# Attention of the second stack: the order of VectorE's steps within a unit

## The chip, the cores and the metric

The kernel runs on one core of one Trainium2 chip. The metric is the device time of one execution in microseconds (us); lower is better.

## What is computed

A two-layer network (the first stack) is followed by a second two-layer stack with latent attention (MLA). Everything is float32; D_MODEL is 1024, there are 256 tokens of the stream and 256 of a context. The part around the change is the attention of the second stack, eight heads, with 64 plain and 32 rotated features in queries and keys and 64 value features:

```python
def attend(q_nope, q_rope, k_nope, k_rope, v):
    s = (jnp.einsum("bqhd,bkhd->bhqk", q_nope, k_nope)
         + jnp.einsum("bqhr,bkr->bhqk", q_rope, k_rope)).astype(jnp.float32) * ATTN_SCALE
    p = jax.nn.softmax(s, axis=-1).astype(v.dtype)
    return jnp.einsum("bhqk,bkhd->bqhd", p, v)
```

In both layers the 256 stream queries attend to stream and context keys together (512 keys). In layer 0 the 256 context queries also attend to the 256 context keys. The result, with a Fourier part and a convolution part, is multiplied by w_out.

## The kernel before

Every engine has its own hand-written, in-order program, and the programs meet through semaphores (`event(...)` and a few others), on whose counts the waits stand. The network is a list of stages. A `Linear` stage streams weight tiles from HBM through a ring of four buffers; ScalarE makes the upper half of a weight (`w_hi`, line 2132), VectorE the rest (`w_lo`, line 2343), and TensorE (PE in the profile) adds three products (line 1896). VectorE makes `w_lo` of the tile that is AHEAD = 3 places ahead (`split`).

The stage `("mla", layer)` computes attention in **units**. A unit is one head with all 256 queries (two tiles of 128) against 512 keys (a long unit) or 256 keys (a short unit). `mla_units` (line 1572) gives layer 0 eight long units and then eight short ones, and layer 1 eight long ones. Layer 0's stage lies at about 1324 to 1378 us of the trace and layer 1's at about 2231 to 2266 us. For unit i the steps are these:

- scores: `mla_scores`, TensorE, line 1633, into two of the four PSUM banks of the weight ring. It waits until the exponents of unit i - 2, which used the same banks, are done.
- maxima: `mla_maxima`, VectorE, lines 1730 and 1732: two row maxima from PSUM, then a small multiplication that makes the bias of the exponents.
- exponents: `exps`, ScalarE, line 1703: two activations that also sum the rows. Each is an ACTIVATE and an ACTIVATION_READ_ACCUMULATOR. They wait for the maxima of unit i.
- scalings: `probabilities`, VectorE, lines 1742 and 1745: the reciprocals of the sums, and two multiplications in place.
- turning: `middle`, TensorE, line 1661: transposes of the weights into PSUM banks 4 and 5, which are single: it waits for the scalings of unit i and for both copies of unit i - 1.
- copies: half of the turned weights by ScalarE (line 1722), half by VectorE (line 1758), both after the turning.
- values: `pair_values`, TensorE, line 1674, once per pair of units, after both copies of the second. Then ScalarE takes the upper half (line 1718) and VectorE the rest (line 1763, the low halves).

TensorE's queue is, for i from 1 on: scores of unit i + 1, for odd i >= 3 the values of pair (i - 3) / 2, turning of unit i - 1. With the last units come four parts of the output product (`mixed_part`, line 1896 again): part 0 before the turning of the last unit but one, part 1 before the turning of the last unit, then part 2, the last values, and part 3. ScalarE's queue (`mla_scalar`, from line 1695) is: exponents of unit i, upper half of a pair, copy of unit i - 1. VectorE's queue is written out in `mla_vector` (line 1734): scalings of unit i - 1, maxima of unit i + 1, copy of unit i - 1, low half of a pair. The scores and maxima of unit 0 are made in the stage before.

Of the kernel before, what the change touches and what calls it, by code (L numbers as in the profile page):

```python
# [360 lines left out]
def build(nc, dram, out, stages):  # L361
# [4 lines left out]
    with ExitStack() as stack:  # L366
# [163 lines left out]
        def event(name):  # L530

            if name not in done:
                done[name] = sem(name)
            return done[name]
# [5 lines left out]
        def cols(c):  # L540
            return slice(c * T, (c + 1) * T)
# [3 lines left out]
        def link(eng, ins, who):  # L545

            steps[who][1] += 1
            ins.then_inc(steps[who][0], 1)
            eng.wait_ge(*steps[who])
# [810 lines left out]
        def mixed_rows(st):  # L1360

            return h_one[0] if st[1] else (h_hi, h_lo)
# [209 lines left out]
        def mla_units(st):  # L1572

            units = [(h, 0, 0, 2 * T) for h in range(HEADS)]
            return units + ([(h, T, T, T) for h in range(HEADS)] if st[1] == 0 else [])

        def mla_base(st):
            return 0 if st[1] == 0 else 16
# [38 lines left out]
        def score_bank(st, i, t):  # L1617

            return (tiles_before(st) + 2 * (i % 2) + t) % RING
# [104 lines left out]
        def mla_maxima(dve, st, i):  # L1724

            V = nc.vector
            nk = mla_units(st)[i][3]
            dve.wait_ge(event("mla_scores"), mla_base(st) + i + 1)
            for t in range(NT):
                last = V.tensor_reduce(stat2[:, i, t:t + 1], ps[:, score_bank(st, i, t), 0:nk], AX_X, ALU.max)  # L1730
            link(dve, last, "dve")
            V.tensor_scalar(stat2[:, i, 2:4], stat2[:, i, 0:2], -MLA_SCALE, None, ALU.mult).then_inc(event("mla_max"), 1)

        def mla_vector(dve, st, split):
            V = nc.vector
            units, b0 = mla_units(st), mla_base(st)
            n = len(units)

            def probabilities(i):
                _, _, _, nk = units[i]  # L1740
                dve.wait_ge(event("mla_exps"), b0 + i + 1)
                link(dve, V.reciprocal(stat2[:, i, 6:8], stat2[:, i, 4:6]), "dve")
                for t in range(NT):
                    p = p2[:, i % 2, t, 0:nk]
                    last = V.tensor_scalar(p, p, stat2[:, i, 6 + t:7 + t], None, ALU.mult)
                last.then_inc(event("mla_probs"), 1)

            for i in range(n + 2):
                if 1 <= i < n + 1:
                    probabilities(i - 1)  # L1750
                if i + 1 < n:
                    mla_maxima(dve, st, i + 1)
                if i == n - 1:
                    split(stages[stages.index(st) + 1], AHEAD)
                if 1 <= i < n + 1:
                    nk = units[i - 1][3]
                    dve.wait_ge(event("mla_turned"), b0 + i)
                    V.tensor_copy(pt2[:, (i - 1) % 3, 0:nk // P, P:T], ps[:, 5, 0:nk].rearrange("p (k n) -> p k n", n=P)).then_inc(event("mla_copied_dve"), 1)
                if i >= 3 and i % 2:
                    b = (i - 3) // 2  # L1760
                    dve.wait_ge(event("mla_hi"), b0 // 2 + b + 1)
                    d = (slice(None), 4 + b % 4, cols(b // 4))
                    V.tensor_tensor(mixed_rows(st)[1][d], ps[:, 6 + b % 2, 0:T], mixed_rows(st)[0][d].bitcast(F32), ALU.subtract).then_inc(s_h, 1)
# [572 lines left out]
        def _(dve):  # L2336
# [274 lines left out]
            for st in stages:  # L2611
# [127 lines left out]
                elif st[0] == "attention":  # L2739
                    attention_vector(dve, st)  # L2740
                elif st[0] == "delta":
                    delta_vector(dve, st, split)
                elif st[0] == "mixer":
                    mixer_vector(dve, st)
                elif st[0] == "mla":
                    mla_vector(dve, st, split)
# [43 lines left out]
```

## Time and profile before

| | us |
|---|---|
| median of 3 runs | 2485.19 |
| lowest and highest | 2482.44 and 2488.31 |
| the profiled execution: its own time | 2484.83 |
| the profiled execution: its span | 2483.0 |
| mean granted TensorE clock in it | 0.996 |

The span is the time from the first to the last instruction that the profile shows; 1.83 us of the execution's time lie around it. In rows of the timeline the first number is the start in us from the span's start, the second the duration in us, then follow engine, line, operation, output and inputs, and in brackets the engine's idle time before it with what ended it.

### The profile page before, as it was taken

How to read it: one execution, taken by the hardware profiler on the slowest of the kernel's cores; microseconds unless marked ns; L12 is line 12 of the kernel's file. 1: busy time of each engine (PE TensorE's matmuls, PEld its weight loads, DVE VectorE, ACT ScalarE, POOL GpSimd, SP SyncE). 2: the span in 40 equal slices, each digit the busy share in tenths (PEclk: the TensorE clock that was granted, in tenths of full speed). 3: DMA queues.
4: the chain of work that ended last, by engine and by line, in shares of the span. 5: the costliest groups of instructions: out<-in, count | busy, mean ns of one | idle time of the engine just before them, and what ended most of it. 6: DMA issues, size and time to landing. Idle time of an engine off the chain costs nothing.

```text
span 2483.0 us, 37020 instructions
## 1 busy us (share of the span) xinstructions
PE 2416.5 (97%) x14770; PEld 2095.3 (84%) x14770; DVE 1761.1 (71%) x3048; ACT 1058.0 (43%) x1684; POOL 59.8 (2%) x56
## 2 busy tenths in 40 slices
PE   6999999999999999999999999999999999999998
PEld 4869999977999988888886888888888888877998
DVE  3668889965778777677768676666866565877666
ACT  4556447742644522222536442222532222555444
POOL 0110001022000000000000000000000000000000
PEclk9999999999999999999999999999999999999999
DMA  8567885533666445554311244444354444432553
GB/s 306 211 249 247 288 273 177 179 136 136 215 210 205 159 163 186 175 181 153 105 36 64 77 153 163 159 166 155 104 180 151 152 144 129 126 102 94 186 184 125
DMA packets 113675, 409.93 MB, mean 165 GB/s; under 512 B 12640, under 2 KB 20064, under 8 KB 108896
## 3 DMA queue, kind: packets, MB, share of 16 engines
q1 hardware_dynamic: 113504, 407.56, 48.6%
q8 instruction: 118, 1.93, 0.3%
q14 instruction: 53, 0.43, 0.0%
HBM read 406.46 MB, written 1.05 MB: 164 GB/s over the span
## 4 chain that ended last, share of the span: by engine, by line
PE 90%; DVE 5%; ACT 2%; DMA 2%; issue 1%; SPq 0%; POOL 0%; DVEq 0%; ACTq 0%
PE ps L1896 77%; PE ps L1918 2%; DVE w_lo L2343 1%; PE ps L605 1%; PE ps L911 1%; DMA first_high<-in_first_rows 1%; PE ps L1674 1%; PE ps L921 1%; PE ps L1661 1%; PE ps L1633 1%; PE ps L1936 1%; ACT w_hi L2132 0%; DVE ssq L2498 0%; DMA raw<-in_tiles 0%; DVE x L2475 0%
## 5 line engine op out<-in xcount | busy, mean ns | idle before, releaser
L2132 ACT CAST w_hi<-raw 128x1024 fp32r<-128x1024 f32 (+3 forms) x557 | 555.1, 997 | 1126.1 <-PE ps L1896 1105.3
L1896 PE MATMUL ps<-h_hi,w_hi 128*128 128x258 f32 (+2 forms) x2928 | 962.5, 329 | 13.4 <-DVE h_lo L2568 4.3
L1896 PE MATMUL ps<-h_lo,w_hi 128*128 128x258 f32 (+2 forms) x2928 | 951.5, 325 | 0.0
L1896 PE MATMUL ps<-h_hi,w_lo 128*128 128x258 f32 (+2 forms) x2928 | 950.4, 325 | 0.0
L2343 DVE TENSOR_TENSOR w_lo<-raw,w_hi 128x1024 fp32r<-128x1024 f32 (+3 forms) x557 | 645.9, 1160 | 273.3 <-ACT w_hi L2132 269.5
L1896 PEld LDWEIGHTS ps<-h_hi,w_hi 128*128 128x128 f32 x2928 | 553.8, 189 | 67.2 <-issue 11.1
L1896 PEld LDWEIGHTS ps<-h_hi,w_lo 128*128 128x128 f32 x2928 | 553.5, 189 | 49.1 <-issue 3.6
L1896 PEld LDWEIGHTS ps<-h_lo,w_hi 128*128 128x128 f32 x2928 | 553.1, 189 | 45.3
L1896 PE MATMUL ps<-a_hi,w_hi 128*128 128x256 f32 (+1 forms) x1056 | 353.5, 335 | 0.5 <-DVE a_lo L2388 0.5
L1896 PE MATMUL ps<-a_hi,w_lo 128*128 128x256 f32 (+1 forms) x1056 | 353.1, 334 | 0.0
L1896 PE MATMUL ps<-a_lo,w_hi 128*128 128x256 f32 (+1 forms) x1056 | 353.1, 334 | 0.0
L1896 PEld LDWEIGHTS ps<-a_lo,w_hi 128*128 128x128 f32 x1056 | 199.9, 189 | 20.5
L1896 PEld LDWEIGHTS ps<-a_hi,w_hi 128*128 128x128 f32 x1056 | 198.2, 188 | 21.7 <-DVE a_lo L2388 1.1
L1896 PEld LDWEIGHTS ps<-a_hi,w_lo 128*128 128x128 f32 x1056 | 198.2, 188 | 20.7
L2360 DVE SCALAR_TENSOR_TENSOR ada_raw<-ada_raw,cond_rows 128x1024 f32<-128x1024 f32 x160 | 195.1, 1219 | 0.0
L2475 DVE SCALAR_TENSOR_TENSOR x<-ps,coef,x 128x256 f32<-128x256 f32 x256 | 116.0, 479 | 96.3 <-PE ps L1896 96.3
L2360 DVE SCALAR_TENSOR_TENSOR ada_acc<-ada_raw,cond_rows 128x1024 f32<-128x1024 f32 x128 | 155.8, 1217 | 0.0
L2463 DVE TENSOR_TENSOR a_f<-silu_g,ps 128x512 f32<-128x512 f32 x64 | 44.0, 687 | 98.0 <-PE ps L1896 61.0
L2439 DVE TENSOR_TENSOR normed<-ps,rstd 128x258 f32<-128x258 f32 x165 | 69.8, 423 | 40.6 <-PE ps L1896 36.2
L2388 DVE TENSOR_TENSOR a_lo<-a_f,a_hi 128x256 fp32r<-128x256 f32 (+1 forms) x132 | 72.9, 552 | 12.0 <-ACT a_hi L2165 12.0
L2165 ACT CAST a_hi<-a_f 128x256 fp32r<-128x256 f32 (+1 forms) x132 | 67.1, 509 | 12.6 <-DVE a_f L2443 12.0
L2191 ACT ACTIVATE h_hi<-x,coef 128x256 fp32r<-128x256 f32 x72 | 34.9, 506 | 28.0 <-DVE x L2475 27.8
(369 smaller groups left out, 2135.7 us busy)
## 6 DMA issues: line engine op xcount, KB each, us to landing
raw<-in_tiles SPq DMA_DIRECT2D x477, 512.0 KB, 3.8
ada_raw<-in_w_mod_by_feature SPq DMA_DIRECT2D x128, 512.0 KB, 3.6
wide_rows<-in_wide_rows SPq DMA_DIRECT2D x32, 1024.0 KB, 4.9
raw<-in_tiles SPq DMA_DIRECT2D x48, 384.0 KB, 3.1
ada_raw<-in_ada_w_by_feature SPq DMA_DIRECT2D x32, 512.0 KB, 4.4
first_low<-in_first_rows SPq DMA_DIRECT2D x2, 2048.0 KB, 13.3
first_high<-in_first_rows SPq DMA_DIRECT2D x2, 2048.0 KB, 21.9
raw<-in_tiles SPq DMA_DIRECT2D x16, 192.0 KB, 2.3
```

The lines of the kernel that those rows point to most:

```text
L605: last = nc.tensor.matmul(ps[32 * j:32 * j + 32, bank, :], cond_wide[:, k, :], wide_one[i % 2][:, HALF * j:HALF * (j + 1)], start=(k == 0) ...
L1896: last = mm(ps[0:m, slot, 0:n], w[:, slot, k * P:k * P + m], v[:, s0 + k, c0:c0 + n], start=(k == 0 and w is w_hi and v is hi), stop=(k == ...
L1918: last = mm(to, w[:, slot, k * P:(k + 1) * P], v[:, k, c * W:(c + 1) * W], start=(k == 0 and w is w_hi and v is hi), stop=(k == KD - 1 and ...
L2132: nc.scalar.copy(w_hi[:, slot, 0:n], raw[:, slot, 0:n]).then_inc(s_hi, 1)
L2165: nc.scalar.copy(a_hi[:, j // 2, a0:a0 + n], a_f[:, (j // 2) % 2, 0:n]).then_inc(s_ahi, 1)
L2191: A(hi[:, j, 0:T], x[:, j, cols(c)], ACT.Identity, scale=coef[:, c, 0, j:j + 1]).then_inc(event("scaled_hi"), 1)
L2343: V.tensor_tensor(w_lo[:, slot, 0:n], raw[:, slot, 0:n], w_hi[:, slot, 0:n].bitcast(F32), ALU.subtract).then_inc(s_lo, 1)
L2360: last = V.scalar_tensor_tensor(out=junk if unit >= SECOND and c == 0 else rows, in0=rows, scalar=1.0, in1=cond_rows[:, c], op0=ALU.mult, ...
L2388: V.tensor_tensor(a_lo[:, pair, a0:a0 + n], a_f[:, pair % 2, 0:n], a_hi[:, pair, a0:a0 + n].bitcast(F32), ALU.subtract).then_inc(s_alo, 1)
L2439: V.tensor_tensor(z, ps[:, slot, 0:W], rstd_2[:, 0], ALU.mult).then_inc(s_evac, 1)
L2463: V.tensor_tensor(a_f[:, pair % 2, 0:n], silu_g[:, pair % 2, 0:n], bank, ALU.mult).then_inc(s_evac, 1 if lin.more["early"] and pair == 1 e ...
L2475: last = V.scalar_tensor_tensor(out=x[:, j, cols(c)], in0=ps[:, slot, cols(c)], scalar=coef[:, c, 2, j:j + 1], in1=x[:, j, cols(c)], op0=A ...
```

## The change

Only the order of VectorE's queue within the attention stage changes. The maxima of unit 1 stay first. Then, in step i, the scalings of unit i (before: of unit i - 1) stand ahead of the maxima of unit i + 1, and the copy of unit i - 1 and the low half come behind them as they did. The scalings of the last unit so come ahead of the `split` of the weight tile instead of behind it.

```diff
+            mla_maxima(dve, st, 1)
             for i in range(n + 2):
-                if 1 <= i < n + 1:
-                    probabilities(i - 1)
-                if i + 1 < n:
+                if i < n:
+                    probabilities(i)
+                if i and i + 1 < n:
                     mla_maxima(dve, st, i + 1)
                 if i == n - 1:
                     split(stages[stages.index(st) + 1], AHEAD)
```

No instruction is added or removed and no transfer is changed. The queues of TensorE, ScalarE and SyncE are untouched.

## Rows read from the trace of the kernel before

**Rows 1.** The page, busy time of each engine.
```profile
PE 2416.5 (97%) x14770; PEld 2095.3 (84%) x14770; DVE 1761.1 (71%) x3048; ACT 1058.0 (43%) x1684; POOL 59.8 (2%) x56
```

**Rows 2.** Waits, 1324 to 1372 us: total, times, longest.
```profile
PE ps L1661 <- DVE p L1745: 4.1, 6, 1.2
```

**Rows 3.** Waits, 2231 to 2263 us, the same columns.
```profile
PE ps L1661 <- DVE p L1745: 1.5, 3, 0.7
```

**Rows 4.** Timeline, long units, PE, ACT and DVE, 1335 to 1344 us.
```profile
1335.33 1.09 PE L1661 MATMUL ps<-consts,p 128*128 128x128 f32 x8
...
1336.94 0.69 ACT L1703 ACTIVATE p<-ps,rstd 128x512 f32<-128x512 f32 x1
...
1337.40 0.15 DVE L1742 RECIPROCAL rstd<-rstd 128x2 f32<-128x2 f32 x1
...
1337.59 0.88 DVE L1745 TENSOR_SCALAR p<-p,rstd 128x512 f32<-128x512 f32 x2
...
1338.18 0.21 ACT L1703 ACTIVATION_READ_ACCUMULATOR p<-ps,rstd 128x1 f32 x1
1338.39 1.28 DVE L1730 TENSOR_REDUCE rstd<-ps 128x1 f32<-128x512 f32 x2
...
1338.53 1.09 PE L1661 MATMUL ps<-consts,p 128*128 128x128 f32 x8 [0.39 <-DVE p L1745]
...
1339.70 0.17 DVE L1732 TENSOR_SCALAR rstd<-rstd 128x2 f32<-128x2 f32 x1
...
1343.15 1.09 PE L1661 MATMUL ps<-consts,p 128*128 128x128 f32 x8
```

**Rows 5.** Timeline, short units, PE, ACT and DVE, 1361 to 1367 us.
```profile
1361.95 0.66 PE L1661 MATMUL ps<-consts,p 128*128 128x128 f32 x4
...
1362.92 0.48 ACT L1703 ACTIVATE p<-ps,rstd 128x256 f32<-128x256 f32 x1
...
1363.73 0.21 ACT L1703 ACTIVATION_READ_ACCUMULATOR p<-ps,rstd 128x1 f32 x1
...
1364.18 0.66 PE L1661 MATMUL ps<-consts,p 128*128 128x128 f32 x4 [0.70 <-DVE p L1745]
...
1365.23 0.16 DVE L1742 RECIPROCAL rstd<-rstd 128x2 f32<-128x2 f32 x1
...
1365.95 0.75 DVE L1730 TENSOR_REDUCE rstd<-ps 128x1 f32<-128x256 f32 x2
...
1366.65 0.66 PE L1661 MATMUL ps<-consts,p 128*128 128x128 f32 x4
1366.74 0.17 DVE L1732 TENSOR_SCALAR rstd<-rstd 128x2 f32<-128x2 f32 x1
```

**Rows 6.** Timeline of ScalarE: exponents of units 1 and 15, then layer 1's 1 and 7.
```profile
1327.44 0.69 ACT L1703 ACTIVATE p<-ps,rstd 128x512 f32<-128x512 f32 x1
...
1369.84 0.48 ACT L1703 ACTIVATE p<-ps,rstd 128x256 f32<-128x256 f32 x1
...
2234.01 0.69 ACT L1703 ACTIVATE p<-ps,rstd 128x512 f32<-128x512 f32 x1
...
2254.52 0.69 ACT L1703 ACTIVATE p<-ps,rstd 128x512 f32<-128x512 f32 x1
```

**Rows 7.** Timeline of TensorE at the end of layer 1's stage.
```profile
2254.95 1.95 PE L1674 MATMUL ps<-pt,v_tok 128*64 128x256 f32 x16 [0.95 <-ACT pt L1722]
...
2261.48 1.09 PE L1661 MATMUL ps<-consts,p 128*128 128x128 f32 x8 [0.68 <-DVE p L1745]
```

**Rows 8.** Timeline of TensorE, two of its longer waits elsewhere.
```profile
390.79 0.39 PE L1896 MATMUL ps<-h_hi,w_hi 128*128 128x258 f32 x1 [1.77 <-DVE h_lo L2568]
...
621.98 0.36 PE L1896 MATMUL ps<-h_hi,w_hi 128*128 128x256 f32 x1 [2.22 <-DVE h_lo L1302]
```

**Rows 9.** Busy time by engine in a stretch; the number after POOL's is the granted clock.
```profile
390.00:395.00 5.00, 3.98 (x16) 3.60 (x17) 3.48 (x8) 3.52 (x6) 0.00 (x0) 0.66 0.61 180
620.00:625.00 5.00, 3.02 (x25) 3.04 (x26) 3.97 (x13) 2.31 (x4) 0.00 (x0) 1.00 0.00 0
```

## The prediction

> **What bounds the kernel now.** I read the page first. TensorE is busy for 97% of the span [rows 1], so outside a few places everything else hides behind it, and a change that touches only VectorE's queue can act only where TensorE waits. The waits of the two attention stages come next. What ends TensorE's idle time there is mostly the scaling of the exponents, for which the turning waits: 4.1 us in layer 0 [rows 2] and 1.5 us in layer 1 [rows 3]. Those 5.6 us are what an earlier scaling could give back at most. The timeline shows how they come about. Between two turnings behind values, that is one pair of long units, lie 1343.15 - 1335.33 = 7.82 us, of which TensorE waits 0.39 [rows 4]; a pair of short units takes 1366.65 - 1361.95 = 4.70 us with a wait of 0.70 [rows 5]. So the period is 3.91 us per long unit and 2.35 us per short one, set by TensorE's own work and a short detour: turning, copy, scaling, turning. The maxima are not on that path, since they stand one unit ahead of the scalings in VectorE's queue.
>
> **What the order changes.** Instructions and durations stay. What matters is a dependence that the new order closes. The exponents of unit i + 1 need its maxima; the maxima of unit i + 1 now stand on VectorE behind the scalings of unit i; and these need the exponents of unit i. Every unit thus runs through exponents, scalings, maxima, exponents, with ScalarE and VectorE by turns and neither ahead of the other. Before, the maxima of unit i + 1 stood behind the scalings of unit i - 1 only, one unit of slack.
>
> **The length of this loop, long unit** [rows 4]. Exponents: from 1336.94 to the end of the second sum, 1338.18 + 0.21 = 1338.39, so 1.45 us. Reciprocal and scalings: from 1337.40 to the start of the next instruction, 1338.39, so 0.99. Maxima: from 1338.39 to 1339.70 + 0.17, so 1.48. Two handoffs between engines; the nearest price is scaling to turning, from 1337.59 + 0.88 = 1338.47 to 1338.53, 0.06 each, and I take 0.05. Sum 1.45 + 0.99 + 1.48 + 0.10 = 4.02 us, against 3.91 now: 0.11 more per unit.
>
> **Short unit** [rows 5]. Exponents 1363.73 + 0.21 - 1362.92 = 1.02; scalings 1365.95 - 1365.23 = 0.72; maxima 1366.74 + 0.17 - 1365.95 = 0.96; handoffs 0.10. Sum 2.80 us, against 2.35: 0.45 more per unit.
>
> **Layer 0.** The loop starts at the exponents of unit 1, at 1327.44, which nothing in the change moves: maxima 1 and scalings 0 keep their order, and the exponents wait for ScalarE's own queue. Those of unit 15 start at 1369.84 now, 42.40 us later [rows 6]. The new way has seven steps out of a long unit and seven out of a short one: 7 x 4.02 + 7 x 2.80 = 47.74 us, 5.34 more. Carrying the three queues forward unit by unit gives two additions. For units 4, 6 and 8 ScalarE is still at its copy when the maxima are ready (about 0.06 each, 0.2 in all). At unit 10, just after the change to short units, the long values of pair 3 come late, ScalarE stands behind them with the upper half and a copy, and the loop is held once for about 0.7 us. So unit 15 starts at about +6.2. The output product's first part begins behind the values of pair 6, which wait for VectorE's copy of unit 13; that copy now stands behind the maxima of unit 15, so it comes as late as they do and hands the +6.2 on. From there TensorE runs back to back as before.
>
> **Layer 1.** Unit 1 starts at 2234.01 and unit 7 at 2254.52, 20.51 us later [rows 6]. Now 6 x 4.02 plus 0.12 for units 4 and 6 = 24.24, 3.7 more. The values of pair 2, which wait 0.95 us for a copy now [rows 7], wait for VectorE's copy of unit 5, behind the maxima of unit 7, and carry the delay on, about +3.8. Then comes a gain: the last turning waits 0.68 us for scalings [rows 7], which now stand ahead of the split and the copy and are long done. Net about +3.1.
>
> **What costs nothing.** The maxima of unit 1 were first in the queue already. The split of the weight tile now stands behind the last scalings; its tile is first read by part 3 of the output product, three parts and two turnings later, and that slack covers a delay of about 1 us. If it did not, each microsecond of it would be one on TensorE. The weight load that waits for this split moves with it; no queue of transfers is otherwise passed. Late next are VectorE's copies: the one of unit i - 1 comes behind the maxima of unit i + 1, so it starts no sooner than 0.05 + 0.99 + 1.48 = 2.5 us after the exponents of unit i end, and TensorE's turning or values wait for it. In this loop TensorE has 7.82 - 0.39 = 7.43 us of work in 8.04, so it has room.
>
> **The clock.** The new gaps of TensorE are longer: carried forward, about 2.3 us ahead of the values of pair 6 in layer 0, about 2.6 ahead of those of pair 2 in layer 1, others 1.6 or less. Elsewhere in this trace a wait of 1.77 us is followed by a stretch at 0.66 granted clock, hence partly at the 1.2 GHz level, and a wait of 2.22 us by none [rows 8, 9]. In the first case 5 us at 0.66 are 5 x 0.34 = 1.7 us of lost full speed. Both long gaps lie just ahead of product parts, where TensorE is the bound, so a fall would be paid. I put one such fall, 1.7 us, into the forecast; none and two are its bounds. The Trainium skill (TensorE: Matmul & The Clock Gate, What's actually happening) says that the throttled state is the default and activity releases it; the first of the two rows agrees, the second does not show it.
>
> **Sum.** 6.2 + 3.1 + 1.7 = 11.0 us. Against the profiled execution's own time this gives 2484.83 + 11.0 = 2495.8; the median of the runs shown is 0.36 higher, within their spread, so I say 2496.
>
> **The rivals.**
> *TensorE stays the bound and the change pays* (faster). Its 7.43 us of work per long pair are near the loop's 8.04, and if the maxima did not hold the exponents, the 5.6 us of waits for scalings would go: 2484.83 - 5.6 = 2479.2. It decides if the loop is shorter than TensorE's work alone, 3.72 us long and (4.70 - 0.70) / 2 = 2.00 us short. The rows give 4.02 and 2.80, so what speaks for it is only that I could have misread a dependence. The Trainium skill (Perfetto Trace Analysis, Optimization Strategy) advises to find the gaps of the contended engine and make what it waits for start sooner, which is what the change does for the scalings; the trace shows such gaps, and the rule says nothing of what is then late.
> *Only the short units lose* (no change). If the long units' loop were covered, by handoffs near nothing, long units would stay at 3.91 and only 7 x 0.45 = 3.2 remain; less the 0.7 at the end of layer 1, 2487.3.
> *TensorE's clock falls often.* With gaps of over 1 us in nearly every pair the lower level might come back again and again. Six falls at 1.7 us instead of one add 8.5: 2504. Against it: the gaps of some 1 us [rows 7] are there now, with a mean granted clock of 0.996 over the whole execution, and part of such a loss would hide behind the loop.
> *The change does not do what it says.* The queues are in order and the loop is written out, so I give this 1 in 100: 2485.
>
> **How the numbers follow.** Forecast 0.85, faster 0.03, only the short units 0.06, many falls 0.05, no effect 0.01. The forecast's own bounds: no fall of the clock (-1.7), two (+1.7), handoffs of 0.03 to 0.08 in 20 steps with two each (-0.8, +1.2), the additions of the carried-forward queues absent or doubled (-0.9, +0.9), and 2 us of scatter of a median either way. I take 2490 to 2502. A measurement of this kernel tells about 0.2%, 5.0 us, from no change; above it lie all but the low end of the forecast and the falls of the clock: slower 0.88. Within it lie the short-units case, the low end and no effect: 0.09. Faster 0.03.
>
> **What the new profile would show.** In steady long units the exponents start every 4.0 to 4.1 us and in short ones every 2.8; each starts within 0.1 us of the end of its maxima, and each reciprocal within 0.1 us of the end of the exponents. VectorE waits for ScalarE's exponents in every unit. TensorE's wait for scalings is gone and replaced by one for VectorE's copy (line 1758). The turning that waited 0.68 us at the end of layer 1 waits no longer. The stretch from the exponents of unit 1 to the output product is 6 us longer in layer 0 and nearly 4 in layer 1; the rest of the trace only moves. Wrong would be: a period of 3.9 us or less in long units, exponents that start long after their maxima, or a time that differs outside the two stages.

## The result, and the profile of the changed kernel

| | before | changed |
|---|---|---|
| median, us | 2485.17 (6 runs, 2482.44 to 2488.31) | 2497.63 (6 runs, 2494.84 to 2499.27) |
| the profiled execution's own time | 2484.83 | 2498.75 |
| span | 2483.0 | 2497.0 |
| mean granted clock | 0.996 | 0.994 |

The changed kernel takes 1.0045 times as long, with a 95% interval of 1.0036 to 1.0055. By the medians that is 12.5 us more. The page shows the same work as [rows 1]; only the span has grown:

```profile
PE 2420.0 (97%) x14770; PEld 2098.7 (84%) x14770; DVE 1764.1 (71%) x3048; ACT 1059.5 (42%) x1684; POOL 60.3 (2%) x56
```

Line numbers behind line 1747 are up by one; the copy of VectorE is now line 1759 and the product line 1897. The waits from 1324 to 1385 us show what the two engines do now (engine and line, then who is waited for, total, times, longest):

```profile
ACT p L1703 <- DVE rstd L1732: 11.6, 10, 2.1
DVE rstd L1742 <- ACT p L1703: 11.6, 15, 1.6
...
PE ps L1674 <- issue: 6.9, 5, 2.1
...
PE ps L1674 <- DVE pt L1759: 2.1, 2, 1.2
PE ps L1661 <- DVE pt L1759: 1.8, 3, 1.2
```

ScalarE waits for the maxima and VectorE for the exponents, each 11.6 us in all, and neither wait stood in the list of before. TensorE no longer waits for the scalings as in [rows 2]. Its waits now stand mostly ahead of values, 9.0 us in all. For 2.1 us of them the profile names VectorE's copy; for the other 6.9 it names nothing (`issue`), and there the timeline has to tell what ended them (below). The timeline of one long unit in steady state answers to [rows 4]:

```profile
1342.20 0.69 ACT L1703 ACTIVATE p<-ps,rstd 128x512 f32<-128x512 f32 x1
...
1343.45 0.21 ACT L1703 ACTIVATION_READ_ACCUMULATOR p<-ps,rstd 128x1 f32 x1
1343.69 0.17 DVE L1742 RECIPROCAL rstd<-rstd 128x2 f32<-128x2 f32 x1 [0.79 <-ACT p L1703]
...
1344.69 1.28 DVE L1730 TENSOR_REDUCE rstd<-ps 128x1 f32<-128x512 f32 x2
1346.01 0.17 DVE L1732 TENSOR_SCALAR rstd<-rstd 128x2 f32<-128x2 f32 x1
...
1346.21 0.69 ACT L1703 ACTIVATE p<-ps,rstd 128x512 f32<-128x512 f32 x1 [1.30 <-DVE rstd L1732]
```

The sums of the exponents end at 1343.66 and the reciprocal starts at 1343.69. The bias of the next exponents ends at 1346.18 and those exponents start at 1346.21. From unit 4 to unit 5 it is one chain without slack, 1346.21 - 1342.20 = 4.01 us from one unit's exponents to the next's. In front of units 4, 6 and 8 there is a little more: ScalarE is still at its copy when the bias is ready, and the step is 4.15 to 4.19 us. A pair of long units so takes 8.20 us, against 7.82 before. Two short units answer to [rows 5]:

```profile
1370.39 0.47 ACT L1703 ACTIVATE p<-ps,rstd 128x256 f32<-128x256 f32 x1 [0.30 <-DVE rstd L1732]
...
1371.44 0.17 DVE L1742 RECIPROCAL rstd<-rstd 128x2 f32<-128x2 f32 x1 [0.43 <-ACT p L1703]
...
1373.16 0.47 ACT L1703 ACTIVATE p<-ps,rstd 128x256 f32<-128x256 f32 x1 [1.30 <-DVE rstd L1732]
```

The step is 2.77 us, but for one of 3.50 into unit 10. The exponents of unit 1 and unit 15 in layer 0 and of units 1 and 7 in layer 1 answer to [rows 6]:

```profile
1330.02 0.69 ACT L1703 ACTIVATE p<-ps,rstd 128x512 f32<-128x512 f32 x1
...
1378.70 0.47 ACT L1703 ACTIVATE p<-ps,rstd 128x256 f32<-128x256 f32 x1 [1.30 <-DVE rstd L1732]
...
2243.03 0.69 ACT L1703 ACTIVATE p<-ps,rstd 128x512 f32<-128x512 f32 x1
...
2267.42 0.69 ACT L1703 ACTIVATE p<-ps,rstd 128x512 f32<-128x512 f32 x1 [1.31 <-DVE rstd L1732]
```

I call the two distances the **stretches**: 48.68 us in layer 0 and 24.39 in layer 1, against 42.40 and 20.51 before. They are taken inside one execution, so what scatters elsewhere does not touch them.

The loop costs most where it starts. In the kernel before, the exponents of units 2 and 3 followed fast, 5.05 us for both in either layer, since the maxima of a unit did not have to wait for the exponents of the one ahead of it. Here are those of layer 1's unit 3, before and changed, 5.05 and 7.99 us behind unit 1:

```profile
2239.06 0.69 ACT L1703 ACTIVATE p<-ps,rstd 128x512 f32<-128x512 f32 x1
```

```profile
2251.02 0.69 ACT L1703 ACTIVATE p<-ps,rstd 128x512 f32<-128x512 f32 x1 [1.60 <-DVE rstd L1732]
```

The stretch is 3.88 us longer in layer 1 and 6.28 in layer 0, and 2.94 us of either are the loss of this head start. The longer steps of the later units give the rest.

Last, TensorE at the end of layer 1's stage, which answers to [rows 7], and the granted clock there:

```profile
2267.29 0.69 DVE L1759 COPY pt<-ps 128x512 f32<-128x512 f32 x1
...
2268.08 3.63 PE L1674 MATMUL ps<-pt,v_tok 128*64 128x256 f32 x16 [2.59 <-issue]
...
2275.46 1.03 PE L1661 MATMUL ps<-consts,p 128*128 128x128 f32 x8
```

```profile
2265.00:2270.00 5.00, 2.41 (x15) 1.68 (x15) 3.97 (x11) 2.03 (x5) 0.00 (x0) 0.82 0.01 3
2270.00:2275.00 5.00, 5.00 (x38) 3.98 (x35) 1.89 (x3) 0.96 (x2) 0.00 (x0) 0.84 0.29 105
```

The wait ahead of the values of pair 2 is 2.59 us. It ends 0.10 us behind VectorE's copy of unit 5 (2267.29 + 0.69 = 2267.98), which stands behind the maxima of unit 7. Behind this wait the clock falls: the values take 3.63 us instead of 1.95, and 5 x (0.18 + 0.16) = 1.7 us of full speed are lost. The last turning waits no longer.

**Where the 13.9 us between the two profiled executions lie.** Up to the exponents of unit 1 in layer 0 the changed kernel is 2.58 us later (1330.02 against 1327.44), before any changed instruction. In layer 0, from there to the last turning, it takes 6.40 us more (56.13 against 49.73). Between the stages 0.04. In layer 1, from the exponents of unit 1 to the last values, 4.89 more (34.83 against 29.94). The rest, 0.1, lies behind. So the change costs 11.3 us here, and 2.6 are scatter of an earlier part.

### The profile page after: what moved, and what is told of

Its sections match the earlier page's. It is cut to its first block, busy times and chain, and to the rows that moved or that the text cites. A ratio compares the mean times of both kernels' runs of the same rounds, so it can differ in the third digit from the quotient of the medians.

```text
span 2497.0 us, 37020 instructions
## 1 busy us (share of the span) xinstructions
PE 2420.0 (97%) x14770; PEld 2098.7 (84%) x14770; DVE 1764.1 (71%) x3048; ACT 1059.5 (42%) x1684; POOL 60.3 (2%) x56
## 3 DMA queue, kind: packets, MB, share of 16 engines
q8 instruction: 118, 1.93, 0.3%
## 4 chain that ended last, share of the span: by engine, by line
PE 89%; DVE 5%; ACT 2%; DMA 2%; issue 1%; SPq 0%; POOL 0%; DVEq 0%; ACTq 0%
PE ps L1897 77%; PE ps L1919 2%; DVE w_lo L2344 1%; PE ps L605 1%; DMA first_high<-in_first_rows 1%; PE ps L911 1%; PE ps L1674 1%; PE ps L921 1%; PE ps L1937 1%; ACT p L1703 1%; PE ps L1661 0%; ACT w_hi L2133 0%; DMA raw<-in_tiles 0%; DVE rstd L1730 0%; DVE ssq L2499 0%
```

## Experiments

The rivals to the loop theory were these: TensorE's work or the clock sets the stages; the late copies of VectorE are the cause; scaling a unit early costs in whatever order. In each profile I read the two stretches; times are medians, and the kernel before ran on the same chips: 2486.61 us beside the first four kernels and 2486.55 beside the second four.

**One: maxima ahead of scalings.**

```diff
             mla_maxima(dve, st, 1)
             for i in range(n + 2):
-                if i < n:
-                    probabilities(i)
                 if i and i + 1 < n:
                     mla_maxima(dve, st, i + 1)
+                if i < n:
+                    probabilities(i)
```

> From the changed kernel, only the maxima of unit i + 1 and the scalings of unit i change places: the maxima no longer stand behind scalings that wait for the exponents of unit i; VectorE's copy stays behind both. Loop theory (exponents, scalings, maxima, exponents by turns): the loop is open, so the stretch from the exponents of unit 1 to those of unit 15 in layer 0 falls from 48.7 us to about 42.2 (42.4 in the kernel before), that from unit 1 to unit 7 in layer 1 from 24.4 to about 20.7, and the time is about 1 us above the kernel before, 2486. Rival, late copies (it is VectorE's copy behind maxima and scalings that holds TensorE): the copy is as late as in the changed kernel, so the stretches stay near 48 and 24 us and the time near 2495 to 2498.

Measured: 2489.09 us, 1.0009 of the kernel before (1.0000 to 1.0019). Its exponents of units 1 and 15 in layer 0:

```profile
1327.16 0.69 ACT L1703 ACTIVATE p<-ps,rstd 128x512 f32<-128x512 f32 x1
...
1369.86 0.47 ACT L1703 ACTIVATE p<-ps,rstd 128x256 f32<-128x256 f32 x1 [0.18 <-DVE rstd L1732]
```

The stretches are 42.70 and 20.95 us (2234.90 to 2255.85 in layer 1). Two steps changed places, and 6.0 of the 6.3 us of layer 0's stretch came back, although the copy still stands behind both. The late copies are not what makes the stretch long. They do make gaps at its end: in layer 1 the values of pair 2 waited 2.34 us, and the clock fell behind that wait as well (0.88 and 0.78 in the two 5 us from 2255, 1.7 us of full speed). With the 0.7 us of the stretches that would account for the 2.5 us by which this kernel's median is above the kernel before; about 1 had been expected.

**Two: copy ahead of maxima.**

```diff
                 if i < n:
                     probabilities(i)
-                if i and i + 1 < n:
-                    mla_maxima(dve, st, i + 1)
-                if i == n - 1:
-                    split(stages[stages.index(st) + 1], AHEAD)
                 if 1 <= i < n + 1:
                     nk = units[i - 1][3]
...
+                if i and i + 1 < n:
+                    mla_maxima(dve, st, i + 1)
+                if i == n - 1:
+                    split(stages[stages.index(st) + 1], AHEAD)
```

> From the changed kernel, VectorE's copy of unit i - 1 moves ahead of the maxima of unit i + 1, behind the scalings of unit i. Loop theory: the copy (0.61 us long, 0.34 short) and its wait for the turning come into the loop, so it gets longer: unit 1 to 15 in layer 0 from 48.7 to about 54 us, unit 1 to 7 in layer 1 from 24.4 to about 27.8, time about 15 us over the kernel before, plus what the clock takes: 2500 to 2503. Late copies: the copy comes 1.4 us earlier in every unit and TensorE's waits for it go, so most of the loss comes back: 2486 to 2490.

Measured: 2505.04 us, 1.0076 (1.0060 to 1.0092). Exponents of units 1 and 15 in layer 0:

```profile
1329.03 0.69 ACT L1703 ACTIVATE p<-ps,rstd 128x512 f32<-128x512 f32 x1
...
1383.67 0.47 ACT L1703 ACTIVATE p<-ps,rstd 128x256 f32<-128x256 f32 x1 [1.82 <-DVE rstd L1732]
```

Stretches of 54.64 and 27.59 us. The copy comes earlier than in the changed kernel and the kernel is slower still, since the copy and its wait for the turning now lie in the loop. The theory of the late copies is out. The time lies 2 us above the expected range although the stretches are as expected; the clock fell behind waits of TensorE at the end of both stages here too (2.43 us in layer 0, 3.48 in layer 1).

**Three and four: a third row maximum, in the changed kernel and in the kernel before.** Both add one line in `mla_maxima`; its result is overwritten by the reciprocal later.

```diff
+            V.tensor_reduce(stat2[:, i, 6:7], ps[:, score_bank(st, i, 0), 0:nk], AX_X, ALU.max)
             for t in range(NT):
                 last = V.tensor_reduce(stat2[:, i, t:t + 1], ps[:, score_bank(st, i, t), 0:nk], AX_X, ALU.max)
```

> The changed kernel with one more row maximum per unit (of tile 0, into a column that the reciprocal overwrites later), about 0.64 us in a long unit and 0.37 in a short one. Loop theory: every microsecond of it lies in the loop: unit 1 to 15 in layer 0 from 48.7 to about 54.5 us, unit 1 to 7 in layer 1 from 24.4 to about 28.0, time about 9.7 us over the changed kernel, 2507. Theory that TensorE's work or its clock sets the stages: the addition is largely hidden, under 3 us.

> The kernel before with the same additional maximum. Loop theory: here the maxima stand a unit ahead and only part of the addition comes through, where VectorE is late with the scalings: unit 1 to 15 in layer 0 from 42.4 to about 44.7 us, unit 1 to 7 in layer 1 from 20.5 to about 22.0, time about 4 us over the kernel before, 2489. If VectorE's work as such bounded both kernels, the addition would cost as much as in the changed kernel, some 10 us.

Measured: 2510.50 us with it in the changed kernel, 12.9 over that kernel's median, and 2489.95 in the kernel before, 3.3 over its own (1.0013, 1.0003 to 1.0022). The exponents of units 1 and 7 in layer 1, first in the changed kernel with the addition, then in the kernel before with it:

```profile
2252.54 0.69 ACT L1703 ACTIVATE p<-ps,rstd 128x512 f32<-128x512 f32 x1
...
2280.12 0.69 ACT L1703 ACTIVATE p<-ps,rstd 128x512 f32<-128x512 f32 x1 [2.21 <-DVE rstd L1733]
```

```profile
2236.86 0.69 ACT L1703 ACTIVATE p<-ps,rstd 128x512 f32<-128x512 f32 x1
...
2258.61 0.69 ACT L1703 ACTIVATE p<-ps,rstd 128x512 f32<-128x512 f32 x1 [0.26 <-DVE rstd L1733]
```

In layer 1 the stretch grew by 27.58 - 24.39 = 3.19 us in the changed kernel and by 21.75 - 20.51 = 1.24 in the kernel before. In layer 0 it grew by 8.65 (57.33) and 1.93 (44.33). So the same addition to VectorE's work costs the stretch 2.6 times as much under the new order in layer 1. Layer 0's ratio of 4.5 holds more than the loop: its 57.33 is 2.8 over what I expected. There TensorE's waits ahead of values had grown to 1.81 and 2.32 us, and the granted clock was lower over twenty microseconds:

```profile
1350.00:1360.00 10.00, 7.68 (x40) 5.05 (x38) 7.22 (x17) 4.34 (x11) 0.00 (x0) 0.84 0.00 0
1360.00:1370.00 10.00, 8.51 (x54) 6.00 (x51) 7.28 (x23) 3.76 (x12) 0.00 (x0) 0.86 0.00 0
```

A slower TensorE makes the copies late enough to hold ScalarE. That this is the whole 2.8 us was not tested.

**Five and six: a product part in the gap, in the changed kernel and in the kernel before.** On TensorE the first part of the output product moves ahead of the values of the last pair but one.

```diff
+                if i == n - 1:
+                    mixed_part(0)
                 if i >= 3 and i % 2:
                     pair_values((i - 3) // 2)
-                if n - 1 <= i < n + 1:
-                    mixed_part(i - n + 1)
+                if i == n:
+                    mixed_part(1)
```

> The changed kernel, with the first part of the output product moved on TensorE ahead of the values of the last pair but one, so that it fills the gap in which TensorE waits for VectorE's copy. Clock theory: in layer 1 that gap falls from 2.6 us to about 1.1, the granted clock stays at full through the end of the stage (0.86 in the changed kernel), and the values of that pair take 1.95 us instead of 3.63; with 3.5 us of filled gaps in both layers the time is about 5 us under the changed kernel, 2492 to 2493. Loop theory beside it: the stretches of the exponents stay at 48.7 and 24.4 us. Rival: the clock falls here for another reason; then the clock stays at about 0.86 and only 3.5 us or less are won, 2494 or more.

> The same move in the kernel before, where the gap is 0.95 us in layer 1 and some 0.6 in layer 0 and the clock stays up: about 1.8 us under the kernel before, 2484 to 2485, with unchanged stretches of 42.4 and 20.5 us. If the move helped by itself and not by filling the gap, it would win as much as in the changed kernel, some 5 us.

Measured: in the changed kernel 2491.30 us, 6.3 under its median (1.0025 of the kernel before, 1.0013 to 1.0036; by the two ratios the move wins 0.0020, or 5.0 us); in the kernel before 2483.99 us, 2.6 under it (0.9991, 0.9982 to 1.0000, so at the edge of what can be told from no change). The values of pair 2 in layer 1 and the clock behind them, in the changed kernel with the move:

```profile
2265.21 1.95 PE L1674 MATMUL ps<-pt,v_tok 128*64 128x256 f32 x16 [1.16 <-issue]
```

```profile
2265.00:2270.00 5.00, 4.79 (x42) 4.18 (x43) 3.29 (x7) 1.96 (x6) 0.00 (x0) 1.00 0.17 36
```

The wait is 1.16 us instead of 2.59, the clock stays full and the values take 1.95 us instead of 3.63. The stretches are unchanged in both kernels: 48.67 and 24.38, and 42.40 and 20.52. So the loop and the clock are two separate costs: the loop is as it was, and the fall of the clock went with the long wait. The trace is of one execution, but the medians agree with it: had the clock fallen all the same, 3.5 us or less were to be won. From unit 1 to the last values layer 1 takes 31.65 us instead of 34.83, and layer 0's way to the last turning 54.20 instead of 56.13, 5.1 less in all, as expected.

**Seven: maxima, copy, scalings, low half**, on top of the move of experiment six. The diff is against the changed kernel. Written out as one row, the queue of the kernel before is maxima of unit i + 1, copy of unit i - 1, in every second step a low half, scalings of unit i. The change puts these scalings ahead of all three, experiment one ahead of copy and low half, this one ahead of the low half alone. So they do not come as early as in the change, though the expectation says so. At the end of the stage copy and scalings also pass the split.

```diff
             mla_maxima(dve, st, 1)
             for i in range(n + 2):
-                if i < n:
-                    probabilities(i)
                 if i and i + 1 < n:
                     mla_maxima(dve, st, i + 1)
-                if i == n - 1:
-                    split(stages[stages.index(st) + 1], AHEAD)
                 if 1 <= i < n + 1:
                     nk = units[i - 1][3]
...
+                if i < n:
+                    probabilities(i)
+                if i == n - 1:
+                    split(stages[stages.index(st) + 1], AHEAD)
```

> From the kernel of the part in the gap, VectorE's order within a step is maxima of unit i + 1, copy of unit i - 1, scalings of unit i, low half: scalings a unit early as in the change, but behind the maxima, so that the loop is open, and behind the copy, for which TensorE waits. Loop theory with the queues carried forward: unit 1 to 15 in layer 0 41.1 us (42.4 before), unit 1 to 7 in layer 1 20.1 (20.5), and with the filled gaps about 4.3 us under the kernel before, 2482; TensorE then waits next to nowhere for scalings or copies in long units. Rival: early scalings are what costs, in whatever order; then the stretches are above 44 and 22 us and the time is above the kernel before.

Measured: 2481.98 us, 0.9983 of the kernel before (0.9974 to 0.9992), the fastest of all and 2.0 us under experiment six. Exponents of units 1 and 15 in layer 0 (two lines further down in this kernel):

```profile
1329.22 0.69 ACT L1705 ACTIVATE p<-ps,rstd 128x512 f32<-128x512 f32 x1
...
1370.41 0.48 ACT L1705 ACTIVATE p<-ps,rstd 128x256 f32<-128x256 f32 x1
```

Stretches of 41.19 and 19.95 us, both shorter than before. TensorE's waits for scalings from 1324 to 1372 us are 2.0 us, half of [rows 2]:

```profile
PE ps L1661 <- DVE p L1747: 2.0, 4, 0.9
```

Scaling earlier is thus no cost in itself; what counts is what the scalings pass. Both stretches together, against the kernel before: past the low half 1.8 us are won, past the copy too (experiment one) 0.7 are lost, past the maxima too (the change) 10.2.

**Eight: the changed order in layer 1 only.**

```diff
-            mla_maxima(dve, st, 1)
+            if st[1] == 1:
+                mla_maxima(dve, st, 1)
             for i in range(n + 2):
-                if i < n:
-                    probabilities(i)
-                if i and i + 1 < n:
+                u = i if st[1] == 1 else i - 1
+                if 0 <= u < n:
+                    probabilities(u)
+                if (i or st[1] == 0) and i + 1 < n:
                     mla_maxima(dve, st, i + 1)
```

> The changed order in layer 1's attention stage alone, the order before in layer 0's. Loop theory: unit 1 to 15 in layer 0 42.4 us as before, unit 1 to 7 in layer 1 24.4 as changed, time about 3.1 us over the kernel before, and 1.7 more where the clock falls there: 2490. A theory that the two stages do not add up (that layer 0's delay causes the one of layer 1, or the clock's fall) expects 20.5 in layer 1 and no fall of the clock, 2486.

Measured: 2491.75 us, 1.0022 (1.0012 to 1.0031), 5.2 us over the kernel before; expected were 4.8. The stretches are 42.40 in layer 0, to the hundredth that of before, and 24.39 in layer 1, to the hundredth that of the changed kernel. The clock falls there again:

```profile
2263.26 3.32 PE L1674 MATMUL ps<-pt,v_tok 128*64 128x256 f32 x16 [2.59 <-issue]
```

Layer 1's cost needs no delay in layer 0, and the two add up.

## Why the prediction was right

**The loop.** It said that exponents, scalings, maxima and the next exponents become one chain: shown by the timeline and by experiments one, two, three and four. Every unit was to start within 0.1 us of the end of its maxima; units 4, 6 and 8 start some 0.2 us behind it. Its terms were 4.02 us per long unit, measured 4.01, and 2.80 per short one, measured 2.77. The handoffs between ScalarE and VectorE, taken as 0.05 us each, measure 0.03 in the long unit shown.

**The two stages.** Layer 0 was to take 6.2 us more and took 6.40. The stretch is 6.28 us longer, and two of the terms in it were off in opposite ways. The steps alone give 7 x 4.01 + 7 x 2.77 = 47.46, 5.06 over 42.40, where 5.34 had been put in; ScalarE at its copy adds 0.5 where 0.2 had been; the hold at unit 10, put at 0.7, is 3.50 - 2.77 = 0.73. So the sum is nearer than its terms, by luck. Another point is easily misread. The prediction gives 0.11 us more per long unit and 0.45 per short one, which would be 3.9 us in layer 0 and 0.7 in layer 1. It is right all the same, since it took its additions from the whole stretches, and these hold the head start of units 2 and 3, which it never names. Layer 1 was to take 3.1 us more without the clock and took 4.89 with it; less the 1.7 us of the clock that is 3.2.

**The clock.** One fall, 1.7 us, had been put in. It came in layer 1, behind a wait of 2.59 us (forecast 2.6), and not in layer 0, whose longest wait in the stage was 2.10 (forecast 2.3). That it would be one, and not none or two, was a choice between bounds and no forecast from a mechanism. Experiment five ties the fall to the wait. The Trainium skill (TensorE: Matmul & The Clock Gate, What's actually happening) says that the throttled state is the default and activity releases it; the trace agrees, with 1.00 behind the wait of 1.16 us and 0.82 and 0.84 from the one of 2.59 us on.

**What was covered.** The split behind the last scalings cost nothing, as said. Part 3 of the product, which reads its tile, starts 4.32 us behind the last turning in layer 0 in both kernels (1390.47 - 1386.15 and 1381.49 - 1377.17), and in layer 1 1.88 us behind the last values against 1.87. From the exponents of unit 15 to the last turning layer 0 takes 7.45 us against 7.33.

**The sum.** 11.0 us was forecast and the profiled executions give 11.3 in the two stages; the medians differ by 12.5, and the interval, 1.0036 to 1.0055 or 8.9 to 13.7 us, holds both. What the prediction had only in its bounds, as 2 us either way, is the scatter that lies ahead of the stages, 2.58 us in the profiled execution.

**The rivals.** TensorE stays the bound: out, for the stretches follow VectorE's queue (experiment three) and not TensorE's. Only the short units lose: out, since layer 1 has long units alone and lost 3.2 us beside the clock. The clock falls often: it did so only in kernels whose loop is longer still. The change does not do what it says: out by the timeline. The hope behind the faster case was real, though. Experiment seven, which holds the move of experiment six, wins 4.6 us by the medians; 42.40 - 41.19 + 20.51 - 19.95 = 1.8 us of that lie in the stretches, which experiment six left as they were. They come from the scalings as well, moved past the low half and not past the maxima.

## What to carry to other kernels

When an instruction that waits for an engine stands in the queue ahead of one that this same engine waits for, the two form a circle. What counts is over how many units it closes. In the kernel before, the maxima of unit i + 1 stood behind the scalings of unit i - 1, and so the same durations, 4.02 us by the prediction's sum, closed only every second unit: about 2.0 us per unit (an estimate, 4.02 / 2), well under TensorE's 3.91. In the changed kernel they close in every unit, the engines run by turns however much slack each has by itself, and 4.01 to 4.19 us replace the 3.91. Any head start that one engine had built up is lost besides, here 2.94 us in each layer. Before moving a step earlier in an in-order queue, write down for every step behind it who waits for it, add up the circle and divide by its units. Where two steps may both come early, put first the one whose input is ready without the other engine.

## What the runs showed of the hardware

The same wait at the same place can bring a fall of the granted clock in one execution and none in another. Behind a wait of 2.22 us at 621.98 the kernel before kept 1.00 [rows 8, 9]; the changed kernel, with the same instructions there and a wait of 2.23 us, had less:

```profile
622.74 0.37 PE L1897 MATMUL ps<-h_hi,w_hi 128*128 128x256 f32 x1 [2.23 <-DVE h_lo L1302]
```

```profile
620.00:625.00 5.00, 2.77 (x16) 2.60 (x15) 4.14 (x12) 1.24 (x2) 0.00 (x0) 0.79 0.00 0
625.00:630.00 5.00, 5.00 (x39) 5.00 (x38) 3.83 (x6) 4.34 (x7) 0.00 (x0) 0.86 0.20 60
```

The two executions were 0.76 us apart at that wait and 2.58 us apart at the first attention stage. This one fall, 5 x (0.21 + 0.14) = 1.75 us, is nearly all of what came on between.

The traces of all ten kernels hold the instructions of this early part, unchanged. In the 10 us from 2 us before the instruction at which the wait ends:

| wait of TensorE, us | near | fell to 0.83 | kept 1.00 |
|---|---|---|---|
| 1.75 to 1.77 | 392 us | 10 traces | none |
| 1.85 to 1.86 | 561 us | 8 | 2 |
| 2.22 to 2.24 | 622 us | 5 | 5 |

Each fall is 10 x 0.17 = 1.7 us of full speed. The length of a wait alone does not tell whether the clock falls: the longest of these three brought the fewest falls. What else decides is not shown here. In the attention stages the waits of 2.34 to 3.48 us at a stage's end brought a fall in all seven cases (layer 1 of the changed kernel and of experiments one, two, three and eight, layer 0 of experiments two and three), the one of 2.10 us in layer 0 of the changed kernel none. So a part of the scatter between runs, as far as these traces tell, is the number of such falls, and waits of TensorE of about 2 us are worth filling where TensorE is the bound behind them.
